# Stream and last modulation vector folded into the four sums of a mixture of experts

## The reference, cut to what matters

```python
h2 = _rmsnorm(x, norm2_g) * (1.0 + sc2) + sh2
x = x + g2 * _moe(h2, ...)          # _moe = shared expert + sum over 8 of 64 experts of gate * swiglu(h2)
h = _rmsnorm(x, final_norm_g)       # end of the first block
u = rms_norm(h, norm_g_2) @ w_in_2  # start of the second
```

## Time and profile before

| | |
|---|---|
| median of three runs | 3908.13 us (3903.12 to 3909.04) |
| profiled execution | 3901.1 us, span 3899.1 us |
| busy share of the span | PE 86%, DVE 60%, ACT 49%, POOL 21% |
| stage out1, last part, until the next stage's first matmul | to 1659.6 us |
| stage routed, first up chunk to last down chunk | 1733.9 to 2714.2 us |
| stage pre up to the first product | 2727.8 to 2826.7 us |

### The profile page before, as it was taken

How to read it: one execution, slowest core, us unless ns; L and a number is a source line. 1 busy time by engine, 2 the same in 40 slices (tenths; PEclk the granted TensorE clock), 3 DMA queues, 4 the chain that set the end, 5 groups by cost and what they waited for, 6 DMA issues and landing times. The chain is left out here.

```text
span 3899.1 us, 89429 instructions
## 1 busy us (share of the span) xinstructions
PE 3356.5 (86%) x33279; PEld 2271.0 (58%) x33279; DVE 2344.9 (60%) x4442; ACT 1917.0 (49%) x2977; POOL 802.1 (21%) x1086
## 2 busy tenths in 40 slices
PE   4999799668888697889989989998799999788689
PEld 0899789656666475533323333332377778666577
DVE  1688688735566475537757767775486663066631
ACT  0577576535555343217757667775322221066520
POOL 4000000046566100522212222221023233100000
PEclk7999899879999698989999999999899999898899
DMA  8354434422232437779899999953834223365352
GB/s 317 87 169 143 159 128 152 158 69 62 59 80 61 160 100 269 140 243 318 247 301 344 345 362 355 293 147 73 271 77 134 71 76 97 107 146 139 105 179 76
DMA packets 576426, 664.84 MB, mean 171 GB/s; under 512 B 117456, under 2 KB 481680, under 8 KB 572928
## 3 DMA queue, kind: packets, MB, share of 16 engines
q1 hardware_dynamic: 550736, 572.45, 46.0%
q0 software_dynamic: 25216, 86.62, 9.0%
q10 hardware_dynamic: 48, 0.05, 0.0%
HBM read 493.08 MB, written 165.94 MB: 169 GB/s over the span
## 5 line engine op out<-in xcount | busy, mean ns | idle before, releaser
L2596 PE MATMUL routed_p_gu<-routed_fixed,routed_x 128*32 128x512 f32 x3840 | 571.9, 599 | 0.0
L2596 PE MATMUL routed_p_gu<-moe_exp_w,routed_x 128*32 x1280 | 570.9, 599 | 0.7 <-DVE routed_fixed L2718 0.7
L2650 ACT COPY routed_fixed<-moe_exp_w 128x1024 f32 x320 | 332.5, 1047 | 224.9 <-DMA moe_exp_w<-in_exp_w_up_dram 96.6
L2718 DVE COPY routed_fixed<-moe_exp_w 128x1024 f32 x640 | 397.9, 680 | 50.3 <-DMA moe_exp_w<-in_exp_w_up_dram 43.9
L544 PE MATMUL front_ps<-front_a_high,front_w_high 128*128 128x320 f32 (+1 forms) x1120 | 363.8, 325 | 16.4 <-DVE front_w_low L797 13.5
L544 PE MATMUL front_ps<-front_a_high,front_w_low 128*128 128x320 f32 (+1 forms) x1120 | 354.7, 317 | 0.0
L544 PE MATMUL front_ps<-front_a_low,front_w_high 128*128 128x320 f32 (+1 forms) x1120 | 354.6, 317 | 0.0
L2596 PEld LDWEIGHTS routed_p_gu<-moe_exp_w,routed_x 128*32 128x32 f32 x1280 | 135.3, 111 | 356.2 <-issue 356.2
L3602 PE MATMUL pre_ps<-pre_a_high,pre_w_high 128*128 128x512 f32 x720 | 288.2, 400 | 13.5 <-ACT pre_xb L3749 6.9
L2730 DVE COPY routed_fixed<-routed_wd 128x1024 f32 x320 | 204.5, 699 | 156.5 <-PE routed_p_gu L2596 60.0
L2611 PE MATMUL routed_p_y<-routed_wd,routed_hT 128*32 x640 | 287.7, 592 | 3.4 <-DVE routed_fixed L2730 3.4
(11 more groups left out here) (543 smaller groups left out, 7484.8 us busy)
## 6 DMA issues: line engine op xcount, KB each, us to landing
moe_exp_w<-in_exp_w_gate_dram SPq DMA_DIRECT2D x64, 1024.0 KB, 12.9
moe_exp_w<-in_exp_w_up_dram SPq DMA_DIRECT2D x64, 1024.0 KB, 15.8
routed_wd<-in_exp_w_down_dram SPq DMA_DIRECT2D x64, 1024.0 KB, 14.7
front_wt<-in_w_in_dram SPq DMA_DIRECT2D x70, 512.0 KB, 4.4
mod_w<-in_w_mod_dram SPq DMA_DIRECT2D x24, 1024.0 KB, 18.2
pre_wt<-in_w_in_dram SPq DMA_DIRECT2D x44, 512.0 KB, 4.0
rw_abrk<-front_rb SPq DMA_DIRECT2D x64, 320.0 KB, 5.0
rwmix_src<-rw_abrk SPq DMA_DIRECT2D x80, 192.0 KB, 2.5
```

Of the source, the lines that this page charges most:

```text
L2596: op = nc.tensor.matmul(p_gu[spot(s), :], x[:, b % 2, k, spot(s)], w, start=(k == 0), stop=(k == KD - 1))
L2650: nc.scalar.copy(fixed[:, place_of(b, c), 0, :], wgu[:, bass.ds(e % WS, 1), c * D:(c + 1) * D].rearrange("p o n -> p (o n)"))\
L2718: op = nc.vector.tensor_copy(fixed[:, place_of(b, c), s - 1, :], wgu[:, bass.ds(es[s] % WS, 1), c * D:(c + 1) * D].rearrange("p o n -> p ( ...
```

## The change

Sum 1 begins as the stream: out1 stores its tile into total instead of x1 and writes zeros only into sums 2 and 3. The modulation vector, broadcast to all partitions (gain_row), is loaded in the stages shared and routed, and every result is multiplied by it there: in shared in DVE's eviction, in routed in one DVE instruction that multiplies by gate and vector and takes the place of ACT's scaling. To make room the ring fixed has R = 3 slots instead of 4. Of the down copies, ACT now makes spots 1 and 2 for m = 0 and spot 1 for m = 1, DVE spot 3 for m = 0 and spots 2 and 3 for m = 1. In both engines' bodies the up copies c = 3 move to the end: on DVE behind the result, on ACT behind the copy of the hidden rows. In pre the stream's tiles and the vector are not loaded; POOL adds parts 2 and 3 into one, PE sums three operands instead of four, ACT and DVE read the sums in PSUM directly, in halves.

```diff
 # out1
-                sp.dma_start(x1[i * P:(i + 1) * P, :], x[:, i % 3, :]).then_inc(x_stored[i % 3], 16)
+                sp.dma_start(total[PART + i * P:PART + (i + 1) * P, :], x[:, i % 3, :]).then_inc(x_stored[i % 3], 16)
-                for j in range(1, SPOTS):
+                for j in range(2, SPOTS):
                     sp.dma_start(total[j * PART + i * P:j * PART + (i + 1) * P, :], none[:, :]).then_inc(none_sent, 16)
 # shared
+            sp.dma_start(gain_row[:, :], gain.broadcast_to([P, D])).then_inc(gain_loaded, 16)
-                nc.vector.tensor_copy(y[:, t, at], pd[:, c % 4, :]).then_inc(y_used, 1)
+                nc.vector.tensor_tensor(y[:, t, at], pd[:, c % 4, :], gain_row[:, at], ALU.mult).then_inc(y_used, 1)
 # routed
-    R = 4
+    R = 3
 # routed, ACT: down copies
-                    nc.scalar.copy(fixed[:, at, 0, :], wd[:, bass.ds(e % WD, 1), m, :].rearrange("p o n -> p (o n)"))\
-                        .then_inc(first_copied, 1)
+                    for s in (1, 2)[:2 - m]:
+                        op = nc.scalar.copy(fixed[:, at, s - 1, :], wd[:, bass.ds(es[s - 1] % WD, 1), m, :].rearrange("p o n -> p (o n)"))
+                    op.then_inc(first_copied, 1)
 # routed, ACT: body
-                    for c in range(1, CH):
+                    for c in range(1, CH - 1):
                         up_copy(e, j + 1, (b + 1) % BS, c)
                 act.wait_ge(h_turned, j + 1)
                 nc.scalar.copy(hT[:].rearrange("p m t -> p (m t)"), p_h[:, 0:MT * P]).then_inc(hT_made, 1)
-                if not begins(j):
-                    result(j - 1, (b - 1) % BS)
+                if not ends(j):
+                    up_copy(e, j + 1, (b + 1) % BS, CH - 1)
 # routed, DVE: down copies, the new result, body
-                    for s, e in zip((2, 3), es):
+                    for s, e in tuple(zip((2, 3), es))[1 - m:]:
+            def result(j, b):
+                if j == 0:
+                    dve.wait_ge(gain_loaded, 16)
+                dve.wait_ge(chunk_done, down_step(j, MT - 1) + 1)
+                nc.vector.scalar_tensor_tensor(y[:, b % 2, :], p_y[:].rearrange("p h n -> p (h n)"), gate[:, b:b + 1],
+                                               gain_row[:, :], ALU.mult, ALU.mult).then_inc(y_made, 1)
-                if not isinstance(j, int) or j >= BS - 1:
-                    dve.wait_ge(y_made, j + 2 - BS)
-                    for c in range(1, CH):
+                    for c in range(1, CH - 1):
                         up_copies(es, j + 1, (b + 1) % BS, c)
+                if not begins(j):
+                    result(j - 1, (b - 1) % BS)
+                if not ends(j):
+                    up_copies(es, j + 1, (b + 1) % BS, CH - 1)
 # pre, SP: no tile(t) and no gain row; POOL
+            def pair(t):
+                pool.wait_ge(parts_ready[t % 2], 16 * SPOTS * (t // 2 + 1))
+                nc.gpsimd.tensor_tensor(parts_t[t % 2][2], parts_t[t % 2][2], parts_t[t % 2][3], ALU.add).then_inc(paired, 1)
 # pre, PE
-                if t >= 1:
-                    pe.wait_ge(part_made, t)
                 for a in range(2):
-                    for j in range(SPOTS):
+                    if t >= 1:
+                        pe.wait_ge(xg_made, 2 * t - 1 + a)
+                    for j in range(SPOTS - 1):
+                        if j == 2:
+                            pe.wait_ge(paired, t + 1)
```

More of the change, by code:

```diff
@@ L2654, in down_copies @@
             def down_copies(j, b):
-                e, last = owner(act, j, 1), owner(act, j, SPOTS - 1)
+                es = owner(act, j, 1), owner(act, j, 2)
+                last = owner(act, j, SPOTS - 1)
                 for w in range(WS):
@@ L2768, in _ @@
             down_copies(NB - 1, BS - 1)
+            result(NB - 1, BS - 1)
 def first_block(nc, consts, i, s):
-    mods, mix, x1 = s["mods"], s["mix"], s["x1"]
+    mods, mix = s["mods"], s["mix"]
     rw, hg = s["rw"], s["hg"]
@@ L2786, in moe_block @@
 def moe_block(nc, consts, i, s):
[L2787 removed]
+    mods = s["mods"]
+    gain = mods[0:1, 5 * D:6 * D]
     with ExitStack() as ctx:
@@ L3548, in _ @@
             sums_of(0)
-            for j, row in enumerate((gain, last_g.rearrange("(o e) -> o e", o=1), norm_g.rearrange("(o e) -> o e", o=1))):
-                sp.dma_start((gain_row, last_row, g_all)[j][:, :], row.broadcast_to([P, D])).then_inc(rows_loaded[min(j, 1)], 16)
-                if j == 0:
-                    tile(0)
-                if j == 1:
-                    sums_of(1)
-            for t in range(1, 4):
-                tile(t)
+            for j, row in enumerate((last_g, norm_g)):
+                sp.dma_start((last_row, g_all)[j][:, :], row.rearrange("(o e) -> o e", o=1).broadcast_to([P, D]))\
+                    .then_inc(rows_loaded[j], 16)
+            sums_of(1)
             for t in range(LAT_TILES + 1):
                 if t + 2 < LAT_TILES:
-                    sp.wait_ge(summed, t + 1)
+                    sp.wait_ge(summed, 2 * t + 2)
                     sums_of(t + 2)
@@ L3586, in _ @@
             nc.gpsimd.memset(lw[:], 0.0).then_inc(zeroed, 1)
+            def pair(t):
+                pool.wait_ge(parts_ready[t % 2], 16 * SPOTS * (t // 2 + 1))
+                nc.gpsimd.tensor_tensor(parts_t[t % 2][2], parts_t[t % 2][2], parts_t[t % 2][3], ALU.add).then_inc(paired, 1)
+            for t in range(LAT_TILES):
+                pair(t)
             for s in range(N):
@@ L3664, in _ @@
                     u = t % 2
-                    act.wait_ge(x_made, t + 1)
-                    act.drain()
-                    nc.scalar.activation(xl[:, :], x_t[t % 4], ACT.Square, scale=D ** -0.5, accum_out=ms[:, u, 0:1])
-                    act.wait_ge(xg_made, t + 1)
+                    for a in range(2):
+                        act.wait_ge(summed, 2 * t + a + 1)
+                        act.drain()
+                        nc.scalar.activation(xl[:, a * BANK:(a + 1) * BANK], ps[:, a, BANK:2 * BANK], ACT.Square, scale=D ** -0.5,
+                                             accum_out=ms[:, u, 6 * a:6 * a + 1]).then_inc(x_squared, 1)
+                    act.wait_ge(xg_made, 2 * t + 2)
                     act.drain()
@@ L3757, in _ @@
         def _(dve):
-            def gained(t):
-                dve.wait_ge(summed, t + 1)
-                for a in range(2):
-                    cols = slice(a * BANK, (a + 1) * BANK)
-                    op = nc.vector.tensor_tensor(spread[:, t % 2, cols], ps[:, a, BANK:2 * BANK], gain_row[:, cols], ALU.mult)
-                op.then_inc(part_made, 1)
             def low(t):
@@ L3770, in _ @@
             dve.wait_ge(rows_loaded[0], 16)
-            gained(0)
             for t in range(LAT_TILES):
                 u = t % 2
-                dve.wait_ge(part_made, t + 1)
-                dve.wait_ge(x_ready[t % 4], 16 * (t // 4 + 1))
-                nc.vector.tensor_tensor(x_t[t % 4], x_t[t % 4], spread[:, t % 2, :], ALU.add).then_inc(x_made, 1)
                 if t >= 2:
                     dve.wait_ge(h_made, t - 1)
-                dve.wait_ge(x_made, t + 1)
-                if t == 0:
-                    dve.wait_ge(rows_loaded[1], 32)
-                nc.vector.tensor_tensor(xv[:, u, :], x_t[t % 4], last_row[:, :], ALU.mult).then_inc(xg_made, 1)
+                for a in range(2):
+                    cols = slice(a * BANK, (a + 1) * BANK)
+                    dve.wait_ge(x_squared, 2 * t + a + 1)
+                    nc.vector.tensor_tensor(xv[:, u, cols], ps[:, a, BANK:2 * BANK], last_row[:, cols], ALU.mult).then_inc(xg_made, 1)
                 if t >= 3:
```

74 lines of the change are left out of this document (34 added, 40 removed).

## The result

The changed kernel takes 4093.9 us (median of 4 runs, 4086.6 to 4106.9) where the kernel before took 3906.5 on the same chip: 1.0493 times as long, 95% interval 1.0475 to 1.0511. The forecast was 3996 (3948 to 4040). The direction was right, and so was the place; but the whole kernel loses 187 us where 88 were forecast, and the routed stage 208 where 119 were.

A forecast was written before the change was run, and what follows sets the result against it. PE, busy 86% of the span, was taken as the bound, with weights too slow in 25 quads. From 3901.1 us, +119 - 24 - 3 + 1 = +93 gave 3994, raised to 3996; range 3948 to 4040.

The forecast's parts named there:

- Step 1: Routed stage: the later c = 3 wait delays the first down copy, pausing PE 1.84 us per quad; period 13.52 us.
- S: Routed stage: moment the up copies c = 3 pass their wait; forecast to move 3.09 us later, to T0 + 2.07.
- T0: Routed stage: start of a quad's first up matmul on PE, the zero from which the forecast counts times.
- Step 2: Routed stage: 54 quads pay 1.84 us each, 25 DMA-bound quads add 20 us; +119 us in all.
- Steps 3 and 4: Pre stage's first product earlier, -24 us; out1 fewer zeros -3, shared 0, start and end of routed +1.
- A: Routed stage: copies keep up, no pause, period stays 11.68 us; whole kernel 3875 us, faster; chance 0.09.
- B: Routed stage: DMA sets the floor in far more than 25 quads, hiding the period; +75, 3950 us; chance 0.06.
- D: Routed stage: DVE's hidden product also comes late, 1 us more per quad; 4060 us; chance 0.07.
- C: Routed stage: the pause in each quad lowers PE's clock to 1.2 GHz for a while; 4150 us; chance 0.03.

The follow-up runs named there:

- e4: Changed kernel with the scatter of a quad's results issued later, behind the quad's last up chunk; 3992.9 us.
- e1: Changed kernel with the ring back at four slots, the rows of results having one buffer instead of two; 3888.8 us.
- e6: Changed kernel with 8 small identity products, read by nothing, behind each quad's up products in PE's pause; 4062.6 us.
- e5: Changed kernel, ring of three kept, with DVE's owner reads and ACT's copy of the turned tokens moved ahead of the c = 3 wait; 3891.0 us.
- e9: Changed kernel with the gather issued about 4 us later and the scatter left in place; 4085.0 us.
- e2: Kernel before the change with only its ring cut from four slots to three; 4104.6 us.
- e7: e1 with SP issuing each set of small parameters one tile later in the pre stage; 3881.8 us.

## Why the prediction was half right

**Step 1, the wait that moves: right in place, failed in one sentence.** S moved to T0 + 2.07, the pause stands ahead of down, nothing gives it back, and ACT is not the later one. In the quads with short loads the forecast was good: period 13.28 for 13.52. The sentence that failed is that the reads "are instruction for instruction the same, so the first down copy starts at T0 + 2.07 + 5.56". The instructions are the same and their surroundings are not. In the kernel before, the last two of DVE's loads of the quad were these:

```profile
L2484 DVEq TENSOR_LOAD <-moe_owner x2: 306/306/307, 2606.1 to 2606.7; - x2
```

The DMA engines began to move the scattered rows at 2608.0, behind them. Moving S by 3.09 us put the first of the two at T0 + 5.6 (2611.1), into those rows, which move from T0 + 4.7 on. The earlier trace rows held the time of the loads, and no row of mine held their neighbour. It cost 68 us in itself (e4 gives back 101 with the clock).

The trace of the kernel before had shown long loads, on the other sequencer. 32 of ACT's 320 owner loads took over 0.6 us there, the longest 1.15 us, and the down products still came at T0 + 6.89 in 75 of 78 quads:

```profile
L2484 ACTq TENSOR_LOAD <-moe_owner x320: 273/281/1145, 1730.1 to 2707.9; - x160
```

**Step 2, how many quads pay.** The +119 for pauses and weights was 126 - 26 = 100. That it came within 19 us is luck, since it stands on a wrong reading: the 25 quads of the earlier trace rows aren't a stretch in which weights set the pace: quad by quad, nearly all are 11.68, and the rest is single quads of 31.3, 16.1 and 24.2 us and three of 12.1 to 13.5 behind these. (the earlier trace rows is the row of the weight loads, PEld; PE itself waited there 33.0 us in 3 pauses.) All 79 quads paid; only the breaks became shorter.

**Steps 3 and 4.** The pre stage's first product comes 77.9 us after the first issue (2941.91 to 3019.78) where it took 98.9: -21.1 for -24. The rest, out1 with shared, I forecast at -3. From the last product of the mix stage (1465.8 before, 1470.2 after) to the first up product (1733.85 and 1735.34) it is 268.0 and 265.1, 2.9 less. The end of routed, forecast at +1 with its start, took more: from quad 79's first up product to the next stage's first issue it is 31.4 before (2696.35 to 2727.78) and 36.2 after (2905.74 to 2941.91). The last products of the mix stage:

```profile
L1646 PE MATMUL hgmix_po<-hgmix_src,hgmix_s x1024: 219/219/241, 1358.6 to 1465.8; 64*64 64x32 f32 x171
```

```profile
L1646 PE MATMUL hgmix_po<-hgmix_src,hgmix_s x1024: 219/219/241, 1361.6 to 1470.2; 64*64 64x32 f32 x171
```

**The rivals.** A is out, and e1 shows what it would have been worth: 3889, near its 3875. B is out: all quads paid, and the DMA share of the stage fell from 0.90 to 0.78. D is out: PE waits at down, not at p_h. C was real and I gave it 0.03. I judged it by a pause of 1.84; with the long load it became 2.5, near the pauses of 2.7 and 3.2 us (up to 2783.91 and 2796.84) behind which the earlier trace rows had shown 0.66. It came in 23 quads, not in 79, at 1.7 us each. The two failures are one chain: the long load made the pause long enough, and e4, which takes only the load away, has no slow quad. The Trainium skill, TensorE: Matmul & The Clock Gate, section HAM oscillation, which the prediction set aside, says that idle gaps between bursts bring the slow level back. e6 agrees with it: filling the gap alone kept the clock at 1.00.

The range counted a step's uncertainty (5.37 or 5.75 us) and not that a step could meet something new at its new time. With the load (+68) and the clock (+39) on top of the sum, 3994 becomes 4101. The profiled execution took 4086.6, mainly because pauses and weights came to 100 and not 119.

## What to carry to other kernels

A ring one place shorter makes a wait later; what it costs is what stands behind that wait in program order. Look at the sequencer's work there, move it ahead of the wait (e5) or find the room elsewhere (e1, by giving up a buffer that has time to spare). When a piece of work slides in time, list what else runs at the new time, DMA issues of other engines above all, before carrying its duration over. And where a pause is forecast on PE, price it twice, as the pause and as the clock behind it, with the pauses of the trace as the measure.

## What was not expected of the hardware

- A sequencer's load of an owner from memory takes 0.30 us, and up to 1.5 on DVE and on ACT (in e1 and e5) when it begins in the first 1.3 us of a scatter's rows and these came within 3 us of the issue. A later scatter (e4) took this away, a later gather (e9) did not.
- A pause of 2.1 to 2.8 us was followed by the lower clock in 23 quads of 61, which cost 1.7 us each time; a pause of up to 2 us in none of 16 here, and in e2, where half of the pauses are 1.98 us, in 4 of them.
- Small products into PSUM that nothing reads won 31 us (e6).
- The instructions ahead of the routed stage are nearly the same in all kernels, yet its first up product came between 1723 us (e7) and 1744 (e2) in the profiled executions. A few microseconds in one profile are no evidence; distances within a stage are.
